# The RWKV scan of one core: the second way's tiles on the other head's partitions, its products on the off-diagonal corners of TensorE's array

## The chip, the core and the metric

The kernel runs on one core of a Trainium2 chip. The metric is the device time of one execution in microseconds (us), lower is better. The core has five engines that run on their own and wait for each other by semaphores: TensorE (PE; PEld is its weight load) multiplies, VectorE (DVE), ScalarE (ACT) and GpSimd (POOL) compute elementwise, and SyncE (SP) here only issues DMA transfers, in the order of its program.

## The reference, cut to what matters

The reference is a chain of five blocks over 512 latent and 256 context tokens of width 1024. The second layer of the last four is an RWKV layer, and the change touches its scan alone. For each of 16 heads of width 64 and each of two ways (forward and backward in time) it computes, token by token:

```
def step(S, inp):
    w_t, k_t, v_t, kk_t, a_t = inp[:5]
    s_kk = einsum('nbhvk,nbhk->nbhv', S, kk_t)
    S = S * w_t[..., None, :] - s_kk[..., :, None] * (kk_t * a_t)[..., None, :] + v_t[..., :, None] * k_t[..., None, :]
    y_t = einsum('nbhvk,nbhk->nbhv', S, inp[5])
    return S, y_t
...
y = ys[0] + flip(ys[1], axis=1)
```

## The kernel before

The scan is done in chunks of 64 tokens (CH), 12 chunks (NC) for the 768 tokens. Two heads stand together as a head pair `m` (8 pairs): head 0 on partitions 0 to 63, head 1 on 64 to 127 (`HEAD`). A pass `n` handles 4 chunks (BATCH) of one pair for both ways `d`; `pos` 0, 1, 2 is its place in the pair, and n = 3m + pos runs from 0 to 23. The second way goes through the chunks backwards (`CHUNK`).

All products of the scan are of 64x64 corners of the 128x128 array. The helper `heads` issues two of them, one for each head, with rows and output columns of the same half: the two corners on the diagonal.

In a pass, `make` on TensorE issues first the two products that VectorE masks (`sums`), then the 128-wide product of term 2 and those that turn terms by an identity, then the token products (term 2 and term 3 by the identity), then the 32x32 products of lines 3470 (`z_sums`) and 3482 (`tt_sums`), which build the inverse of a chunk's triangular matrix from two blocks, then W (`w_sums`) and the corrections (`corrected`). Between these stand the four steps (`step`) of the pass before: `new`, the state after a chunk, which VectorE scales by the chunk's decay (line 3649) and hands to the next step, and `y_sum`, the output, which VectorE adds to `y` after the fourth step (line 3658). ScalarE copies products from PSUM (line 3544). In a pair's second and third pass the layer norm of the pair before is mixed in: mean and variance (line 3506), centre (3666), squares and roots on ScalarE, reciprocals (3671) and scale (3676, 3678) on VectorE.

SP loads what a pass needs, in one queue, in this order for a pair: the blocks from which GpSimd will compute the next inverse, the terms of the first pass, the inverse (two stores to DRAM, a wait until they have landed, twelve loads), the terms of the second and the third pass. The terms of a pass are five parts, and each is issued when the one before has landed:

```
for part in range(PARTS):
    w = slice(part * LOAD, part * LOAD + LOAD)
    sp.dma_start(self.terms[b][:, w], src[:, w]).then_inc(self.landed, 16)
    sp.wait_ge(self.landed, (48 * m + 16 * b - 16) * PARTS + 16 * part + 16)
sp.sem_inc(self.ready, 1)
```

Before the first part SP waits on `taken`, by which VectorE says that the pass that used the buffer is over; three buffers are in turn. A pass on TensorE begins with a wait on `ready` (SP's line 3328). GpSimd computes the inverse of the next pair (lines 2816 to 2819, 3404) and, after `scaled`, the layer's output for a pair three back (3389, 3391).

Of the kernel before, what the change touches and what calls it, by code (L numbers as in the profile page):

```python
# [21 lines left out]
D = 1024  # L22
KD = D // P
# [24 lines left out]
CH = 64  # L48
# [3136 lines left out]
class RwkvScan(Stage):  # L3185
# [5 lines left out]
    def __init__(self, chip, before):  # L3191
# [16 lines left out]
        self.state = [chip.view(at + 2 * d * CH, 2, CH) for d in range(2)]  # L3208
        at += 4 * CH
# [9 lines left out]
        assert at <= self.masks_at, at  # L3219
        assert D + 2 * BLK * BLK <= WSLOT  # L3220
# [16 lines left out]
                "state_ready state_sums y_sums y_added made").split())  # L3237

# [64 lines left out]
    def y_sum(self, s, d):  # L3303

        return self.chip.bank(6, CH, BATCH * CH * d + CH * self.step(s, d))

    def new(self, s, d):

        return self.chip.bank(7, CH, CH * d)
# [6 lines left out]
    def sync(self, sp):  # L3316
        d, b4 = self.chip.dram, self.before
        sp.wait_ge(self.chip.stage_done, 4 * self.index)

        def terms(m, b):  # L3320
# [7 lines left out]
            sp.sem_inc(self.ready, 1)  # L3328

        def inverse(m):  # L3330
# [12 lines left out]
            for way in range(2):  # L3343
                chunks = slice(NC * way, NC * way + NC)
                for q in range(4):
                    to = slice(BLK * q, BLK * q + BLK)
# [7 lines left out]

        inverse(0)
        for u in range(2):
            sp.wait_ge(b4.bonus_stored[u], 16 * (KD // 2))
# [53 lines left out]
    def tensor(self, pe):  # L3411
# [14 lines left out]

        flat = lambda x: lambda s: x[:, s].rearrange("p n e -> p (n e)")
        at = lambda x: lambda s: x[:, s]
        id64 = lambda s: ident

        def make(n, m, pos, past):
            if n == 0:
                wait(self.before.first_terms, 16)
            else:
                wait(self.ready, n)
            for d in range(2):
                x = self.source(pos, d)
                term = lambda i: lambda s: x[:, s, i]
                if past:
                    wait(self.w_out[d], n)  # L3440
                each(at(self.half(d, 1, 0)), term(0), term(3))
                each(at(self.half(d, 1, 1)), term(3), term(1)).then_inc(self.sums[d], 1)
            for d in range(2):
                x = self.source(pos, d)
                pq = lambda s: x[:, s, 0:2].rearrange("p n e -> p (n e)")
                term = lambda i: lambda s: x[:, s, i]
                wait(self.made[d], n + 1)
                each(flat(self.slots(d, 0, 2)), term(2), pq).then_inc(self.sums[d], 1)
                each(at(self.half(d, 2, 0)), term(0), id64)
# [327 lines left out]
```

## Time and profile before

| what | value |
|---|---|
| median of 3 runs | 5429.38 us (5427.31 to 5431.54) |
| the profiled execution's span | 5432.6 us |
| share of PE busy | 88% |
| share of DVE busy | 49% |
| the scan's 64-wide products (line 3419) | 10752 records, first at 3388.7 us, last at 3905.2 us |

The profile is of one execution, whose span of 5432.6 us is its own time, 3 us above the median. All times in it count from the start of the span. PEclk is the granted share of TensorE's full clock. A product of fp32 operands leaves two matmul records and two weight loads.

### The profile page before, as it was taken

The page shows a single profiled execution, that of the slowest core. Times are in us where ns is not written, and L with a number is a line of the kernel's source. Part 1 is how long each engine was busy: PE and PEld are TensorE (multiplying, and loading weights), DVE is VectorE, ACT ScalarE, POOL GpSimd, SP SyncE. Part 2 cuts the span into 40 slices and gives each one's busy share as a digit, 9 for nine tenths or more (in the row PEclk, how much of TensorE's full clock was granted, in tenths as well). Part 3 has the DMA queues.
Part 4 walks back from the last instruction along what each step waited for, and adds up shares of the span by engine and source line. Part 5 has one row for each costly group of instructions (what it writes and reads, how often), then busy time and mean ns, then how long its engine had stood idle before and what let it go on. Part 6 is the DMA issues. An engine that isn't in the chain of part 4 may idle for free.

```text
span 5432.6 us, 72151 instructions
## 1 busy us (share of the span) xinstructions
PE 4768.6 (88%) x28910; PEld 2998.1 (55%) x28910; DVE 2667.7 (49%) x4575; ACT 1230.6 (23%) x2249; POOL 761.8 (14%) x942
## 2 busy tenths in 40 slices
PE   6987888889989989999879943899888999999998
PEld 3555734444478634555445522789744445456687
DVE  2447853441278411477565487345533444423465
ACT  2112412340011010111010164222212343301230
POOL 0004410000000000111000056656100000000000
PEclk9989998889999999999989966999998999999999
DMA  3312141012122211344103255344211100022122
GB/s 142 102 55 101 40 162 54 31 39 93 62 70 86 79 69 39 109 154 162 59 33 104 87 190 209 98 108 109 78 47 43 35 35 31 13 85 78 69 83 78
DMA packets 152502, 451.24 MB, mean 83 GB/s; under 512 B 73200, under 2 KB 73456, under 8 KB 130800
## 3 DMA queue, kind: packets, MB, share of 16 engines
q1 hardware_dynamic: 128464, 350.91, 19.1%
q0 software_dynamic: 22848, 92.29, 5.0%
q8 instruction: 231, 3.78, 0.3%
q10 hardware_dynamic: 864, 3.47, 0.2%
q14 instruction: 95, 0.78, 0.1%
HBM read 377.42 MB, written 69.21 MB: 82 GB/s over the span
## 4 chain that ended last, share of the span: by engine, by line
PE 61%; issue 9%; DVE 8%; POOLq 7%; PEld 7%; DMA 3%; ACT 2%; POOL 2%; DVEq 1%; PEldq 0%; SPq 0%; ACTq 0%
PE psum L386 50%; PEld psum L386 6%; POOLq L2819 3%; POOLq L2817 2%; PE psum L2380 2%; PE psum L2379 2%; PE psum L648 1%; PE psum L2350 1%; DVE sbuf L1091 1%; PE psum L1275 1%; DVE sbuf L663 1%; PE psum L1029 1%; PE psum L1246 1%; DVE sbuf L666 1%; DVE sbuf L1394 1%
## 5 line engine op out<-in xcount | busy, mean ns | idle before, releaser
L386 PE MATMUL psum<-sbuf 128*128 128x512 f32 (+3 forms) x10256 | 3313.4, 483 | 204.0 <-DVE sbuf L1584 52.0
L386 PEld LDWEIGHTS psum<-sbuf 128*128 128x128 f32 (+1 forms) x10256 | 1937.8, 191 | 1539.4 <-issue 1205.6
L3419 PE MATMUL psum<-sbuf 64*64 64x64 f32 (+1 forms) x10752 | 432.1, 240 | 32.2 <-SPq L3328 21.9
L3419 PEld LDWEIGHTS psum<-sbuf 64*64 64x64 f32 x10752 | 418.0, 140 | 48.9 <-SPq L3328 23.8
L598 DVE CUSTOM_DVE_ANT_0 sbuf<-sbuf 128x1024 f32<-128x1024 f32 x160 | 210.9, 1318 | 42.9 <-DMA sbuf<-w_side 27.2
L1596 DVE SCALAR_TENSOR_TENSOR sbuf<-psum,sbuf 128x256 f32<-128x256 f32 (+2 forms) x288 | 125.8, 480 | 191.1 <-PE psum L386 186.4
L3014 PE MATMUL psum<-sbuf 64*128 64x512 f32 (+2 forms) x192 | 86.5, 712 | 144.1 <-ACT sbuf L3088 66.3
L3544 ACT ACTIVATE sbuf<-psum 128x256 f32<-128x256 f32 (+3 forms) x384 | 128.4, 368 | 370.9 <-PE psum L3419 311.8
L631 ACT ACTIVATE sbuf<-sbuf 128x512 f32<-128x512 f32 (+1 forms) x114 | 52.9, 552 | 617.1 <-DVEq L3718 599.9
L588 POOL DMA_DIRECT2D sbuf<-w_side x128 | 68.4, 535 | 858.6 <-DVE sbuf L598 857.9
L2818 POOL TENSOR_TENSOR sbuf<-sbuf 96x30 f32<-96x30 f32 (+14 forms) x240 | 140.6, 586 | 50.9 <-issue 18.0
L3014 PEld LDWEIGHTS psum<-sbuf 64*128 64x128 f32 (+1 forms) x192 | 39.5, 265 | 187.0 <-POOL sbuf L2976 69.6
L1853 DVE TENSOR_TENSOR sbuf<-sbuf 128x512 f32<-128x512 f32 x40 | 27.8, 694 | 227.3 <-ACT sbuf L1843 227.3
L555 POOL DMA_DIRECT2D sbuf<-cond_rows x4 | 2.4, 603 | 940.0 <-DVEq L3718 856.8
L2816 POOL TENSOR_TENSOR sbuf<-sbuf 96x30 f32<-96x30 f32 (+14 forms) x240 | 125.9, 524 | 33.7 <-issue 1.7
L1459 DVE TENSOR_TENSOR sbuf<-sbuf,psum 128x512 f32<-128x512 f32 x16 | 10.3, 685 | 240.5 <-PE psum L386 240.5
L2524 DVE TENSOR_REDUCE sbuf<-psum 128x1 f32<-128x768 f32 x64 | 61.3, 958 | 135.8 <-PE psum L2380 134.2
L648 PE MATMUL psum<-sbuf 128*128 128x512 f32 (+1 forms) x228 | 93.0, 566 | 29.8 <-ACT sbuf L631 29.8
L3649 DVE TENSOR_SCALAR sbuf<-psum,sbuf 128x64 f32<-128x64 f32 x192 | 45.9, 280 | 147.4 <-PE psum L3419 145.8
L2477 POOL TENSOR_TENSOR sbuf<-sbuf 64x512 f32<-64x512 f32 x16 | 20.3, 1267 | 689.1 <-ACT sbuf L2412 446.1
L2380 PE MATMUL psum<-sbuf 64*128 64x512 f32 (+1 forms) x256 | 116.4, 534 | 0.0
L1584 DVE TENSOR_TENSOR sbuf<-sbuf 128x1024 f32<-128x1024 f32 (+1 forms) x100 | 100.1, 1005 | 29.0 <-DMA sbuf<-w_sgu_out 10.8
(309 smaller groups left out, 5174.2 us busy)
## 6 DMA issues: line engine op xcount, KB each, us to landing
sbuf<-w_side POOLq DMA_DIRECT2D x128, 512.0 KB, 3.9
sbuf<-w_sgu_uz SPq DMA_DIRECT2D x32, 1088.0 KB, 5.1
sbuf<-terms SPq DMA_DIRECT2D x115, 256.0 KB, 2.9
sbuf<-w_up SPq DMA_DIRECT2D x22, 1024.0 KB, 4.9
sbuf<-w_merge SPq DMA_DIRECT2D x8, 2560.0 KB, 8.9
sbuf<-w_mla_head SPq DMA_DIRECT2D x16, 1152.0 KB, 5.1
sbuf<-w_sgu_v SPq DMA_DIRECT2D x8, 2048.0 KB, 7.7
sbuf<-w_sgu_out SPq DMA_DIRECT2D x8, 2048.0 KB, 8.6
```

What stands on the lines that cost most here:

```text
L386: last = nc.tensor.matmul(out, w, x, start=(n == 0), stop=(n == len(pairs) - 1))
L598: last = v.tensor_tensor_reduce(junk, self.slot[b], self.rows[:, c], 1.0, 0.0, ALU.mult, ALU.add, self.sums[:, b, n:n + 1])
L648: last = self.nc.tensor.matmul(self.chip.bank(n, t), self.chip.const("ones"), squares[:, i], start=(i == 0), stop=(i == k - 1))
L1596: last = v.scalar_tensor_tensor(x[:, m], self.chip.bank(i)[:, cols], gates[sign][:, m:m + 1], x[:, m], ALU.mult, ALU.add)
L2379: t.matmul(s[:, a:a + w], self.qn[u][:, q], self.kn[u][:, a:a + w], start=True, stop=False)
L2380: last = t.matmul(s[:, a:a + w], rot[r, q], self.kr[u][r, a:a + w], start=False, stop=True)
L2816: engine.tensor_tensor(product, left, right, ALU.mult)
L2818: engine.tensor_tensor(x[:, j + 1:BLK, 0:j], x[:, j + 1:BLK, 0:j], product, ALU.add)
L2819: eng.drain()
L3014: last = t.matmul(out[:, at:at + width], w, x[:, at:at + width], start=True, stop=True)
L3419: last = t.matmul(out[hs], lhs[hs], rhs[hs], start=start, stop=stop)
L3544: copy = lambda to, of: a.activation(to, of, ACT.Copy)
```

## The change

The second way's (d = 1) results stand on the partitions of the other head. `heads` takes `turned`: with 1, head h is read on its own rows and written to the other half, an off-diagonal corner. The new helper `corners` issues, for each chunk, the first way's two products on the diagonal and then the second way's two off it. All products that read the terms go through it; those on already turned tiles (W, the corrections, `new`) stay on the diagonal, and the y products turn the second way back. The y products leave `step` for `outputs`, one block between W and the corrections of the next pass, and the add to `y` moves behind that pass's corrections. The states of all four steps get buffers of their own, y and state sums other places in banks 6 and 7. Since the queries and decays of the second way are read by VectorE on the partitions of the other head, SP loads them once more, crossed: `turned` behind each pass's terms, and two loads of decays at the stage's start. The inverse's loads for the second way go to swapped partitions; their number stays.

```diff
+        def turned(m, b):
+            sp.wait_ge(self.turned_in, 32 * (3 * m + b) + 32)
+            q = d["terms"][3 * m + b, :, 1].rearrange("p (c n e) -> p c n e", n=TERMS, e=CH)[:, :, 1]
+            for h in range(2):
+                sp.dma_start(self.queries[b][HEAD[h]], q[HEAD[1 - h]]).then_inc(self.turned_in, 16)
...
             sp.sem_inc(self.ready, 1)
+            turned(m, b)
...
+        for h in range(2):
+            sp.dma_start(self.decays_turned[HEAD[h]], b4.decays[HEAD[1 - h], :, 1]).then_inc(self.turned_in, 16)
         inverse(0)
+        turned(0, 0)
...
-        def heads(out, lhs, rhs, start=True, stop=True):
-            for hs in HEAD:
-                last = t.matmul(out[hs], lhs[hs], rhs[hs], start=start, stop=stop)
+        def heads(out, lhs, rhs, turned=0, start=True, stop=True):
+            for h in range(2):
+                rows = HEAD[h]
+                last = t.matmul(out[HEAD[h ^ turned]], lhs[rows], rhs[rows], start=start, stop=stop)
             return last
...
+        def corners(out, lhs, rhs, done=None):
+
+            for s in range(BATCH):
+                last = [heads(out(d)(s), lhs(d)(s), rhs(d)(s), turned=d) for d in range(2)]
+            if done is not None:
+                for d in range(2):
+                    last[d].then_inc(done[d], 1)
...
-                each(at(self.half(d, 1, 0)), term(0), term(3))
-                each(at(self.half(d, 1, 1)), term(3), term(1)).then_inc(self.sums[d], 1)
+            corners(half(1, 0), term(0), term(3))
+            corners(half(1, 1), term(3), term(1), self.sums)
...
+            corners(lambda d: flat(self.slots(d, 0, 2)), term(2), pq, self.sums)
+            corners(half(2, 0), term(0), id64)
+            corners(half(2, 1), term(4), id64, self.sums)
...
+            corners(half(0, 0), term(2), id64)
+            corners(half(0, 1), term(3), id64, self.token_sums)
...
+            if past:
+                outputs(*past)
             for d in range(2):
                 wait(self.tokens_out[d], n + 1)
                 wait(self.w_out[d], n + 1)
...
+        def outputs(n, m, pos):
+            v = self.v[pos]
             for d in range(2):
-                c = self.step(s, d)
-                heads(self.y_sum(s, d), v[d][:, c], self.nh_h[d][:, c, 0], stop=False)
-                heads(self.y_sum(s, d), self.state[d][:, s % 2], self.qa[d][:, c], start=False).then_inc(self.y_sums[d], 1)
+                wait(self.state_ready[d], 13 * m + 4 * pos + BATCH + 1)
+            for s in range(BATCH):
+                for d in range(2):
+                    c = self.step(s, d)
+                    heads(self.y_sum(s, d), v[d][:, c], self.nh_h[d][:, c, 0], turned=d, stop=False)
+                for d in range(2):
+                    c = self.step(s, d)
+                    last = heads(self.y_sum(s, d), self.state_at(n, s, d), self.qa[d][:, c], turned=d, start=False)
+                    if s + 1 == BATCH:
+                        last.then_inc(self.y_sums[d], 1)
...
-                v.tensor_tensor(self.qa[d], x[:, :, 1], c1[:, :, 0], sub)
+                if d == 1:
+                    dve.wait_ge(self.turned_in, 32 * n + 64)
+                v.tensor_tensor(self.qa[d], x[:, :, 1] if d == 0 else self.queries[pos], c1[:, :, 0], sub)
...
             dve.sem_inc(self.taken, 1)
+            if past:
+                add_outputs(*past)
```

SP's queue of DMA transfers at the start of the scan, before (line 3326 loads a part of terms, 3348 and 3349 the inverse, 3353 the blocks):

```order
L3349 DMA sbuf<-inverse 32x12x32
L3326 DMA sbuf<-terms 128x512 x5
L2953 DMA blocks<-sbuf 32x24x32 x4
L3353 DMA sbuf<-blocks 96x1024
L3326 DMA sbuf<-terms 128x512 x5
L3353 DMA sbuf<-blocks 96x1024
L3326 DMA sbuf<-terms 128x512 x5
L3339 DMA inverse<-sbuf 96x1024
L3340 DMA inverse<-sbuf 96x1024
```

and the same place of the changed kernel, where these lines are 3343 (terms), 3368 (inverse), 3372 (blocks) and 3357, 3358 (stores), and 3335 is the new load of queries:

```order
L3368 DMA sbuf<-inverse 32x12x32
L3335 DMA sbuf<-terms 64x4x64 x2
L3343 DMA sbuf<-terms 128x512 x5
L3335 DMA sbuf<-terms 64x4x64 x2
L2953 DMA blocks<-sbuf 32x24x32 x4
L3372 DMA sbuf<-blocks 96x1024
L3343 DMA sbuf<-terms 128x512 x5
L3335 DMA sbuf<-terms 64x4x64 x2
L3372 DMA sbuf<-blocks 96x1024
L3343 DMA sbuf<-terms 128x512 x5
L3335 DMA sbuf<-terms 64x4x64 x2
L3357 DMA inverse<-sbuf 96x1024
```

Two loads more stand behind each pass's terms and ahead of the next transfer: two pairs of them are ahead of the first load of blocks from which GpSimd works.

VectorE's operations from the last steps of a third pass on, before (3649 scales the states, 3658 adds to y, 3671 is a reciprocal, 3629 to 3632 take in the corrections):

```order
L3649 TENSOR_SCALAR sbuf<-psum,sbuf 128x64 x8
L3658 TENSOR_TENSOR sbuf<-sbuf,psum 128x256 x2
L3671 RECIPROCAL sbuf<-sbuf 128x384
L3629 TENSOR_TENSOR sbuf<-sbuf,psum 128x512
L3631 TENSOR_TENSOR sbuf<-sbuf,psum 128x256
L3632 TENSOR_TENSOR sbuf<-sbuf,psum 128x256
```

and of the changed kernel, where the same lines are 3695, 3705, 3718, 3670, 3674 and 3675:

```order
L3695 TENSOR_SCALAR sbuf<-psum,sbuf 128x64 x8
L3718 RECIPROCAL sbuf<-sbuf 128x384
L3670 TENSOR_TENSOR sbuf<-sbuf,psum 128x512
L3674 TENSOR_TENSOR sbuf<-sbuf,psum 128x256
L3675 TENSOR_TENSOR sbuf<-sbuf,psum 128x256
```

The add to y no longer stands between the states and the corrections; it comes after the corrections of both ways, ahead of the next pass's masks.

## Rows read from the trace of the kernel before

**Rows 1.** The page: span, TensorE, and the scan's products.
```profile
span 5432.6 us, 72151 instructions
PE 4768.6 (88%) x28910; PEld 2998.1 (55%) x28910; DVE 2667.7 (49%) x4575; ACT 1230.6 (23%) x2249; POOL 761.8 (14%) x942
L3419 PE MATMUL psum<-sbuf 64*64 64x64 f32 (+1 forms) x10752 | 432.1, 240 | 32.2 <-SPq L3328 21.9
```

**Rows 2.** Stretches: start and end, length, busy us of engines, clock, DMA.
```profile
3704.00:3764.00 60.00, 59.22 (x1619) 55.34 (x1615) 32.90 (x83) 19.60 (x57) 39.35 (x72) 1.00 0.42 112
...
3868.00:3925.00 57.00, 36.49 (x782) 32.12 (x780) 32.43 (x59) 10.25 (x25) 13.06 (x10) 0.86 0.19 67
```

**Rows 3.** Waits of 3524 to 3868 us: total, times, longest.
```profile
PE psum L3419 <- SPq L3328: 14.3, 5, 4.2
```

**Rows 4.** All waits of SP over the scan, 3388 to 3910 us.
```profile
SPq L3326 <- DMA sbuf<-terms: 257.4, 92, 4.1
SPq L3328 <- DMA sbuf<-terms: 60.9, 23, 4.0
SPq L3348 <- DMA inverse<-sbuf: 26.7, 7, 4.6
SPq L3338 <- POOLq L3405: 11.4, 1, 11.4
SPq L3334 <- DVEq L3592: 4.9, 1, 4.9
```

**Rows 5.** SP in order of time: start, us, transfers, over two head pairs.
```profile
3630.46 0.33 SPq L3353 DMA_DIRECT2D sbuf<-blocks  x1
...
3659.74 25.39 SPq L3326 DMA_DIRECT2D sbuf<-terms  x10
3688.31 0.33 SPq L3353 DMA_DIRECT2D sbuf<-blocks  x1
...
3747.77 0.33 SPq L3353 DMA_DIRECT2D sbuf<-blocks  x1
```

**Rows 6.** In order of time, TensorE and (L3605) VectorE: second passes of two pairs.
```profile
3673.80 9.43 PE L3419 MATMUL psum<-sbuf 64*64 64x64 f32 x288 [0.83 <-SPq L3328]
3683.16 0.45 PE L3470 MATMUL psum<-sbuf 32*32 32x32 f32 x32
...
3675.00 0.43 DVE L3605 TENSOR_TENSOR sbuf<-psum,sbuf 128x256 f32<-128x256 f32 x1 [0.16 <-PE psum L3419]
...
3853.51 11.01 PE L3419 MATMUL psum<-sbuf 64*64 64x64 f32 x288 [2.68 <-SPq L3328]
```

**Rows 7.** Line 3419 alone: 64-wide products only, then 128-wide ones only.
```profile
3679.00:3682.00 3.00, 3.00 (x110) 3.00 (x107) 1.00 0.34 93
3669.50:3672.50 3.00, 3.00 (x60) 3.00 (x58) 1.00 0.39 126
```

**Rows 8.** Line 3055 alone (tiles of 64 rows, 32 columns), one stretch.
```profile
3366.00:3367.00 1.00, 1.00 (x136) 1.00 (x131) 1.00 0.00 0
```

**Rows 9.** SP's issues by line: issue ns min/median/max; the parts' landing.
```profile
L3349 SPq DMA_DIRECT2D sbuf<-inverse x64: 469/471/1429, 3391.2 to 3838.9; - x64
L3326 SPq DMA_DIRECT2D sbuf<-terms x115: 319/320/1920, 3398.8 to 3865.1; - x115
DMA to landing us min/median/max: 2.5/2.9/4.5
```

**Rows 10.** The end of the scan in order of time and one group by line.
```profile
3868.19 1.43 SPq L363 DMA_DIRECT2D sbuf<-w_rwkv_out  x2
...
3876.45 0.43 DVE L3605 TENSOR_TENSOR sbuf<-psum,sbuf 128x256 f32<-128x256 f32 x1 [0.30 <-PE psum L3419]
3896.55 2.55 DVE L3671 RECIPROCAL sbuf<-sbuf 128x384 f32<-128x384 f32 x1 [0.30 <-issue]
...
3905.58 0.94 DVE L3658 TENSOR_TENSOR sbuf<-sbuf,psum 128x256 f32<-128x256 f32 x2 [0.28 <-PE psum L3419]
...
L3544 ACT ACTIVATE sbuf<-psum 128x256 f32<-128x256 f32 (+3 forms) x384 | 128.4, 368 | 370.9 <-PE psum L3419 311.8 <-PE psum L3470 30.1 <-PE psum L3482 27.9
```

More of the change, by code:

```diff
@@ L3219, in __init__ @@
         assert at <= self.masks_at, at
+        at = A_W + WSLOT + D + 2 * BLK * BLK
+        self.queries = [chip.view(at + b * BATCH * CH, BATCH, CH) for b in range(BATCHES)]
+        at += BATCHES * BATCH * CH
+        self.decays_turned, at = chip.view(at, KD, NC), at + KD * NC
+        self.state = [chip.view(at + d * 2 * BATCH * CH, 2 * BATCH, CH) for d in range(2)]
+        at += 4 * BATCH * CH
+        assert at <= A_W + 2 * WSLOT, at
         assert D + 2 * BLK * BLK <= WSLOT
@@ L3303, in y_sum, with state_at @@
     def y_sum(self, s, d):
-        return self.chip.bank(6, CH, BATCH * CH * d + CH * self.step(s, d))
+        return self.chip.bank(6 + d, CH, CH * self.step(s, d))
     def new(self, s, d):
-        return self.chip.bank(7, CH, CH * d)
+        return self.chip.bank(6, CH, BATCH * CH + CH * d)
+    def state_at(self, n, s, d):
+        i = BATCH * n + s
+        return self.state[d][:, i % (2 * BATCH)]
     def step(self, s, d):
@@ L3453, in make @@
             for d in range(2):
-                x = self.source(pos, d)
-                term = lambda i: lambda s: x[:, s, i]
                 wait(self.evacuated[d], 2 * n + 2)
-                each(at(self.half(d, 0, 0)), term(2), id64)
-                each(at(self.half(d, 0, 1)), term(3), id64).then_inc(self.token_sums[d], 1)
+            corners(half(0, 0), term(2), id64)
+            corners(half(0, 1), term(3), id64, self.token_sums)
             if past:
@@ L3537, in alone @@
                 step(*past, s)
+            outputs(*past)
             mean(KD - 1)
@@ L3639, in begin @@
                 for d in range(2):
-                    v.memset(self.state[d][:, 0], 0.0)
+                    v.memset(self.state_at(n, 0, d), 0.0)
                     dve.drain().then_inc(self.state_ready[d], 1)
@@ L3647, in step, with add_outputs @@
             for d in range(2):
-                at = m * (2 * NC) + NC * d + self.step(s, d) + self.CHUNK[pos][d]
-                v.tensor_scalar(self.state[d][:, 1 - s % 2], self.new(s, d), self.decays[:, at:at + 1], None, mult
+                at = self.step(s, d) + self.CHUNK[pos][d]
+                decay = (self.before.decays[:, m, 0] if d == 0 else self.decays_turned[:, m])[:, at:at + 1]
+                v.tensor_scalar(self.state_at(n, s + 1, d), self.new(s, d), decay, None, mult
                                 ).then_inc(self.state_ready[d], 1)
-            if s + 1 == BATCH:
-                if n == 0:
-                    dve.wait_ge(self.zeroed, 1)
-                for d in range(2):
-                    dve.wait_ge(self.y_sums[d], 4 * n + 4)
-                for d in range(2):
-                    y = self.y[:, m * NC + self.CHUNK[pos][d]:m * NC + self.CHUNK[pos][d] + BATCH]
-                    v.tensor_tensor(y, y, self.chip.bank(6, BATCH * CH, BATCH * CH * d).rearrange("p (c e) -> p c e", e=CH), add).then_inc(self.y_added[d], 1)
-                    dve.drain()
+        def add_outputs(n, m, pos):
+            if n == 0:
+                dve.wait_ge(self.zeroed, 1)
+            for d in range(2):
+                dve.wait_ge(self.y_sums[d], n + 1)
+            for d in range(2):
+                y = self.y[:, m * NC + self.CHUNK[pos][d]:m * NC + self.CHUNK[pos][d] + BATCH]
+                v.tensor_tensor(y, y, self.chip.bank(6 + d, BATCH * CH).rearrange("p (c e) -> p c e", e=CH), add).then_inc(self.y_added[d], 1)
+                dve.drain()
         def centre(m):
@@ L3684, in alone @@
                 step(n, m, pos, s)
+            add_outputs(n, m, pos)
             centre(m)
```

28 lines of the change are left out of this document (12 added, 16 removed).

## The prediction, made blind

> **What bounds the kernel now.** I read the page first, for how much of the span the scan's products are. Line 3419 holds all 64-wide products of the scan, 10752 matmul records busy 432 us, first at 3388.7 us and the last at 3905 us [rows 1]. Everything the change touches lies in this stage of some 537 us, a tenth of the span. A product of fp32 operands leaves two records, so these are 5376 products over 24 passes.
>
> Then the stretches. TensorE is busy 59.22 of 60.00 us between 3704 and 3764, at the full clock [rows 2]. That invites the reading that the products set the pace. The list of waits warns against it: between 3524 and 3868 TensorE's longest waits end at SP's line 3328, 14.3 us in 5 times [rows 3]. Line 3328 is where SP says that a pass's terms have landed.
>
> So I read SP's own waits, and this is what decides [rows 4]. Over the scan SP waits 257.4 + 60.9 us for its own loads of terms and 26.7 us for its own stores of the inverse. It waits only once each for another engine: 11.4 us for GpSimd's first inverse and 4.9 us for VectorE's memset. It never waits for `taken`, the semaphore by which the passes would hold it back. In order of time the same shows [rows 5]: a head pair is a load of blocks, five parts of terms one after the other, two stores and twelve loads of the inverse, then ten parts. The next load of blocks comes 57.9 us later (3630.46 to 3688.31) and the one after that 59.5 us later. Nothing in between is idle but landing time. SP runs free at some 58 to 60 us a head pair, and TensorE needs a little less: its three passes fit, with 0.83 us of waiting at 3673.80 and 2.68 us at 3853.51, each at a pair's second pass, the one behind the loads of the inverse [rows 6]. Two chains stand almost level, and SP's is the slower one.
>
> **The change, part by part.**
>
> *Products on all four corners.* A 64-wide product on the diagonal costs 3.22 us / 110 = 29.3 ns a record (a 3 us stretch that holds 110, the last one running 0.22 us over), a 128-wide one 3.27/60 = 54.5 ns [rows 7]. Two corners take turns. The trace has no four corners of 64x64. The nearest row is line 3055: tiles of 64 rows and 32 columns, of which two share each half of the rows, in the same order of halves as the new code. At full clock 136 records overlap 1.00 us, 1.19/136 = 8.8 ns each [rows 8]. Line 3470, with four 32x32 tiles that share no rows, takes (0.45-0.19)/31 = 8.4 ns [rows 6]. So sharing rows costs nothing there. I take half of today's spacing for corners: 14.7 and 27.3 ns. Per pass 192 records of 64 columns, 32 of 128 and the 64 records of y move to corners: 2.8 + 0.9 + 0.9 = 4.6 us less TensorE work in a pass. The bounds are 0 (no overlap) and 5.9 us (spacing down to line 3055's).
>
> The Trainium skill speaks against this ("TensorE: Matmul & The Clock Gate", Part 3): a weight load overlaps products in flight only where its row group differs, and an off-diagonal corner shares its rows with a diagonal one. By that rule the corners would gain nothing; line 3055's spacing here disagrees, for 32 columns. It is a rival below.
>
> *SP gets two more loads in each pass.* `turned` stands behind each pass's terms and ahead of all that SP does next: 64 partitions x 4 runs of 256 bytes, 256 runs, twice. SP's issue of a part of terms (128 runs) takes 0.32 us, of an inverse load (384 runs) 0.47 us, both with outliers to 1.9 us [rows 9]. I take 0.42 us with its gap, so 0.84 for two, 0.1 for the semaphore steps (`turned` waits for the pair before it, landed long ago), and 0.3 because the next part queues behind 512 small runs (parts land in 2.5 to 4.5 us, 2.9 in the median, so a little more traffic is felt). That is 1.25 us a pass. Bounds: 0.75 (twice 0.32 and the steps) and 1.9.
>
> Which of them count? Those of passes 4 to 22 stand after SP's one wait for GpSimd and ahead of the last pass's terms: 19 x 1.25 = 23.8 us. Those of passes 0 and 1 stand ahead of the load of blocks from which GpSimd makes the first inverse, on which SP waits 11.4 us, so they pass through: 2.4 us. Those of passes 2 and 3 vanish in that wait. The two loads of decays lie in the 4.9 us that SP waits for the memset. The last pass's terms land 26.2 us later (bounds 15.8 and 40).
>
> *y products in one block, late; add to y after the corrections.* They leave the four steps of state and stand between W and the corrections. Cover: SP's 15.6 us or more between passes. In the last pass and the steps after it they are bare.
>
> *What is given back at the end.* Today SP's last terms are in at 3868.2 (its next load goes out then), while VectorE's first mask of the last pass is at 3876.45, and it follows the start of the pass by 1.2 us as at 3673.80 to 3675.00 [rows 6, 10]. The pass starts at 3875.2, 7.0 us late, because TensorE lags. Shorter passes take this lag away where they fit between SP's arrivals: the second pass of a pair gets 15.6 us (14.3 + 1.25). I lay a pass out by durations of today [rows 10]. After 1 us of first products, eight masks and evacuations of up to 0.43 us on VectorE hold the token products back to 3.7 us, ScalarE's copies of 0.37 us hold z to 6 us, the small products with their copies, variance and roots end at 10.3, W 1.75, y 0.9, corrections 3.45: 16.4 us. I leave 1.5 us of lag. VectorE then needs 1.2 + 0.94 (the moved add) + 2.55 (reciprocal): 21.1 us, where it is 23.9 today (3875.2 to 3899.1, where today's reciprocal ends). So 2.8 us less. The y products of the last batch cost 1.8 us more behind the last state: 64 records at twice 14.7 ns, since TensorE idles between these steps and the granted clock of this stretch averages 0.86, part of it at the lower of the two levels, 1.2 GHz in place of 2.4 [rows 2]. Given back: 7.0 - 1.5 + 2.8 - 1.8 = 6.5 us (bounds 3 and 10).
>
> **The sum.** 26.2 - 6.5 = 19.7 us more. The profiled execution has a span of 5432.6 us, 3 us above the median of 5429.4, and the difference carries over: 5449 us. The middle of the scan gains nothing: where a pass takes 16 us in place of 19, TensorE waits longer at SP's line.
>
> **The rivals.**
>
> *Corners that don't overlap*: the second product on a half of the rows waits for the first, passes stay at 19 us, TensorE keeps its lag, SP's 18 x 1.25 + 2.4 = 24.9 us reach the 22nd pass, which today already waits for its terms (2.68 us), and all behind it shifts alike, with 1.8 us of y on top: +26.7, 5456 us. Against it: line 3055. For it: nothing in this trace has 64-column weights on shared rows at this pace. Chance 0.10. The rule of the Trainium skill quoted above would have it so.
>
> *The loads are cheap*: 0.8 us a pass and 9 us given back, 16.8 - 9 = +8 us, 5437 us, within what can be told. For it: the 0.32 us issues. This and smaller mixtures: 0.27.
>
> *The products set the pace after all*, the other side: were SP not the slower chain, each pass would lose some 3.5 us, 24 x 3.5 = 84 us, 5345 us. For it speak the 59.22 of 60.00 busy us. The point from which it decides: SP's three sets of terms, inverse and extra loads would have to take under the 47 us of three shortened passes, and they take 58 and more. For a gain that can be measured at all, `turned` would have to cost under 0 us beside the lag, or the parts land 0.3 us sooner each. Chance 0.07, and 0.02 for small gains.
>
> *Cold TensorE*: gaps at each first pass grow to some 10 us (z waits for the inverse, about 16 us behind the terms), and after idle stretches like that of 3868 to 3925 the granted clock averages 0.86 [rows 2]. A cold last pass would take back up to 6 us. This lies inside my forecast's range.
>
> **How the numbers follow.** My forecast, SP's chain longer and part of it given back, has 0.54 and by itself 5440 to 5462. What a measurement of this kernel tells from no change is about 0.2%, 11 us. Slower by over that: 0.54 + 0.10, less 0.02 for its edge, 0.62. Within: 0.29. Faster: 0.09. The range 5431 to 5466 leaves out the fast case, the dearest loads (40 - 3 = +37) and little else.
>
> **What would show it.** SP's loads of blocks 61 to 64 us apart, in place of 58 to 60, and still no wait for `taken`. TensorE's busy time in the scan down by some 100 us, its waits that end at SP's ready line between the second inverse and the last terms up from 14.3 us to over 60. Records of corner products half as far apart. Passes in step with SP: the last one starting within 2 us of the last terms. It would be wrong if SP waited for passes, if the query loads' issue took under 0.3 us each, or if part loads went faster with TensorE idle.

## The result, and the profile after

The changed kernel takes 5465.9 us (median; runs of 5460.0 to 5467.9 us) against 5428.4 us for the kernel before in the same job. The ratio is 1.0067, with a 95% interval of 1.0054 to 1.0081: slower by some 36 us (the two medians are 37.5 us apart). One more execution of it, and one of e2 below, ran at a granted clock under 0.7 (8757 and 6946 us) and are left out. The forecast was 5449 us and the range 5431 to 5466: the time lies inside by 0.1 us, and the loss is nearly twice the 19.7 us that were forecast.

The page of the kernel after answers to [rows 1]. SP's waits and TensorE's waits over the scan answer to [rows 4] and [rows 3]. The lines are renumbered: 3343 is the wait for a part of terms (3326 before), 3345 that for the last part (3328), 3335 the new query loads, 3356 the wait for GpSimd, 3372 the load of blocks (3353), 3442 the 64-wide products (3419), 3498 the product z with the inverse (3470), 3536 the sums of mean and variance (3506).

```profile
span 5466.1 us, 72297 instructions
L3442 PE MATMUL psum<-sbuf 64*64 64x64 f32 (+1 forms) x10752 | 348.1, 248 | 77.6 <-SPq L3345 21.6
```

SP's own waits, 3380 to 3960 us: engine and line, what it waited for, us in total, times, longest.

```profile
SPq L3343 <- DMA sbuf<-terms: 259.1, 92, 6.0
SPq L3345 <- DMA sbuf<-terms: 59.5, 23, 4.0
SPq L3367 <- DMA inverse<-sbuf: 24.4, 7, 3.9
SPq L3356 <- POOLq L3427: 7.7, 1, 7.7
```

TensorE's waits in the same stretch:

```profile
PE psum L3498 <- DMA sbuf<-inverse: 56.0, 8, 14.7
PE psum L3442 <- SPq L3345: 21.6, 10, 5.6
PE psum L3442 <- issue: 19.0, 17, 3.0
PE psum L3442 <- DVE sbuf L3652: 15.8, 17, 1.7
```

Read together: SP waits for the same things for the same time as before and never for `taken`, so it still runs free. The products are 84 us less busy (348.1 for 432.1), and TensorE stands still for all of it and for the 31 us by which the stage is longer. SP in order of time shows what is new in its round:

```profile
3581.62 0.60 SPq L3372 DMA_DIRECT2D sbuf<-blocks  x1
...
3648.01 0.62 SPq L3335 DMA_DIRECT2D sbuf<-terms  x1
3648.67 0.60 SPq L3372 DMA_DIRECT2D sbuf<-blocks  x1
...
3666.11 1.25 SPq L3335 DMA_DIRECT2D sbuf<-terms  x2
3667.41 0.61 SPq L3357 DMA_DIRECT2D inverse<-sbuf  x1
...
3709.80 0.60 SPq L3372 DMA_DIRECT2D sbuf<-blocks  x1
```

A query load takes 0.6 us to issue, two of them hold the queue for 1.30 us (3666.11 to 3667.41), and the load of blocks that follows takes 0.60 us where it took 0.33 [rows 5]. The blocks are 67.1 and 61.1 us apart.

The stage's end, TensorE in order of time (start, us, records, in brackets the idle time ahead and what ended it):

```profile
3909.46 0.69 PE L3442 MATMUL psum<-sbuf 64*64 64x64 f32 x32 [0.76 <-DVE sbuf L3652]
3913.13 1.97 PE L3442 MATMUL psum<-sbuf 64*64 64x64 f32 x48 [2.97 <-issue]
3915.03 0.65 PE L3498 MATMUL psum<-sbuf 32*32 32x32 f32 x32
...
3917.46 2.42 PE L3536 MATMUL psum<-sbuf 128*128 128x384 f32 x4
...
3936.52 1.12 PE L3442 MATMUL psum<-sbuf 64*64 64x64 f32 x16 [0.73 <-DVE sbuf L3695]
3938.37 1.99 PE L3442 MATMUL psum<-sbuf 64*64 64x64 f32 x64 [0.73 <-DVE sbuf L3695]
```

And as stretches (length, then busy us of TensorE, its weight loads, VectorE, ScalarE, GpSimd; granted clock; DMA). Before, the last pass from its first record to VectorE's last subtraction, then from there to the stage's end (the first addition of line 1584):

```profile
3875.16:3896.24 21.08, 19.54 (x520) 18.01 (x516) 11.55 (x28) 6.22 (x18) 2.93 (x3) 1.00 0.13 44
3896.24:3924.42 28.18, 9.83 (x136) 7.79 (x136) 14.57 (x21) 1.72 (x3) 8.32 (x6) 0.72 0.08 28
```

After:

```profile
3904.63:3928.07 23.44, 18.38 (x516) 15.93 (x516) 11.32 (x28) 6.02 (x18) 1.21 (x3) 0.85 0.36 131
3928.07:3961.34 33.27, 12.29 (x136) 8.02 (x136) 15.41 (x22) 1.72 (x3) 8.32 (x6) 0.57 0.07 24
```

The last pass is 2.4 us longer and what follows it 5.1 us longer, each at a lower clock than before.

**The account.** SP has the last pass's terms in at 3904.5 us, 36.8 us later than before. 5.4 us of that lie ahead of the scan, in code that the change leaves alone (the scan began at 3394.1 in place of 3388.7 in these two executions), so SP's chain is 31.4 us longer. TensorE's lag at the last pass is gone (it starts 0.1 us behind its terms, 7.4 before): -7.3. Last pass +2.4, tail +5.1. Sum +31.6, and the stage ends 31.5 us later against its start. The rest of the 36 us is of the size by which the code ahead varies between executions.

### The profile page after: what moved, and what is told of

Its sections match the earlier page's. It is cut to its first block, busy times and chain, and to the rows that moved or that the text cites. A ratio compares the mean times of both kernels' runs of the same rounds, so it can differ in the third digit from the quotient of the medians.

```text
span 5466.1 us, 72297 instructions
## 1 busy us (share of the span) xinstructions
PE 4703.1 (86%) x28910; PEld 2920.8 (53%) x28910; DVE 2665.7 (49%) x4575; ACT 1226.1 (22%) x2249; POOL 764.1 (14%) x942
## 4 chain that ended last, share of the span: by engine, by line
PE 60%; issue 10%; DVE 8%; POOLq 7%; PEld 7%; DMA 3%; ACT 2%; DVEq 1%; POOL 1%; PEldq 1%; SPq 0%; ACTq 0%
PE psum L386 48%; PEld psum L386 6%; POOLq L2819 3%; POOLq L2817 2%; PE psum L2380 2%; PE psum L2379 2%; PE psum L648 1%; PE psum L2350 1%; DVE sbuf L1091 1%; PE psum L1275 1%; DMA sbuf<-w_side 1%; DVE sbuf L663 1%; PE psum L1029 1%; PE psum L1246 1%; DVE sbuf L666 1%
## 5 line engine op out<-in xcount | busy, mean ns | idle before, releaser
L3442 PE MATMUL psum<-sbuf 64*64 64x64 f32 (+1 forms) x10752 | 348.1, 248 | 77.6 <-SPq L3345 21.6
L3442 PEld LDWEIGHTS psum<-sbuf 64*64 64x64 f32 x10752 | 329.0, 145 | 102.3 <-issue 37.5
```

The costliest lines, as they stand in the source:

```text
L3442: last = t.matmul(out[HEAD[h ^ turned]], lhs[rows], rhs[rows], start=start, stop=stop)
```

## The experiments

The theory: SP's serial queue sets the pace, the query loads lengthen it, and all that the corners save turns into waiting. The rival: the off-diagonal corners, the order of the products or the late y products are what costs. In the table, *pass* is the mean distance of VectorE's first masks from pass 5 to pass 23, *tail* the time from the end of VectorE's last subtraction to the stage's end, both from the profiled execution.

| kernel | median us | ratio to before, 95% | pass us | tail us |
|---|---|---|---|---|
| before | 5428 to 5433 | | 20.36 | 28.2 |
| after | 5465.9 | 1.0067 (1.0054 to 1.0081) | 21.31 | 33.3 |
| e1 after, no query loads | 5435.1 | 1.0006 (0.9997 to 1.0015) | 19.75 | 32.7 |
| e2 before, with the loads | 5468.1 | 1.0066 (1.0053 to 1.0079) | 22.08 | 27.3 |
| e3 after, parts in flight | 5421.9 | 0.9979 (0.9970 to 0.9989) | 19.57 | 33.3 |
| e4 before, parts in flight | 5413.2 | 0.9967 (0.9954 to 0.9980) | 20.04 | 28.3 |
| e5 after, loads on ScalarE | 5432.7 | 1.0004 (0.9995 to 1.0013) | 20.37 | 32.9 |
| e6 = e3 and e5 | 5419.7 | 0.9983 (0.9974 to 0.9992) | 19.92 | 32.6 |
| e7 = e6 on the diagonal | 5434.3 | 1.0009 (0.9999 to 1.0019) | 20.19 | 34.4 |
| e8 = e6, way by way | 5416.2 | 0.9972 (0.9961 to 0.9982) | 19.41 | 32.9 |
| e9 after, filled tail | 5461.3 | 1.0050 (1.0034 to 1.0065) | 21.48 | 29.0 |
| e10 after, y in its steps | 5456.0 | 1.0039 (1.0024 to 1.0055) | 21.85 | 31.0 |
| e11 = e8, e9 and e10 | 5410.0 | 0.9959 (0.9946 to 0.9973) | 19.28 | 28.4 |
| e12 = e4 and filled tail | 5412.8 | 0.9961 (0.9948 to 0.9975) | 20.11 | 26.7 |

**e1: the loads taken out of the change.**

```diff
             sp.sem_inc(self.ready, 1)
-            turned(m, b)
...
         inverse(0)
-        turned(0, 0)
...
```

> The changed kernel without the two query loads that SP issues in each pass; VectorE takes the queries from the other half of the partitions, so the second way's output is of the wrong queries, and the work on every engine stays the same. The loads of the turned decays stay. Theory (SP's serial queue sets the pace, and each pass's two query loads lengthen it by 1.3 us): the last pass's terms are in 24 to 28 us earlier than in the changed kernel (3904.49 us there), the loads of blocks are again 57 to 60 us apart, and the time falls to 5438 to 5442 us. Rival 1 (off-diagonal corners, the interleaving or the later y products cost the time): the loads of blocks come as now, or the passes hold SP, and the time stays above 5460 us. Rival 2 (all is the loads, and the end gives back the 6.5 us of the prediction once SP is free): 5430 us or less.

Measured: 5435.1 us, the time of the kernel before within what can be told, and 2.9 us below my 5438 to 5442. SP's loads of blocks, in order of time, are 60.1 and 59.5 us apart and take 0.33 us again:

```profile
3568.54 0.33 SPq L3371 DMA_DIRECT2D sbuf<-blocks  x1
...
3628.60 0.33 SPq L3371 DMA_DIRECT2D sbuf<-blocks  x1
...
3688.05 0.33 SPq L3371 DMA_DIRECT2D sbuf<-blocks  x1
```

Rival 1 falls: with corners, order and late y products in place and the query loads gone, the loss is gone. The last terms come 36.7 us sooner (3867.8), more than the 24 to 28 I gave it; 2.6 us of that lie ahead of the scan, so SP's chain is 34.1 us shorter. Rival 2 falls too: with SP free there is no gain either. The end takes it: from the last pass's first mask to the stage's end it takes 54.2 us, as after the change (54.5), where the kernel before takes 48.0.

**e2: the loads alone, on the kernel before.**

```diff
...
             sp.sem_inc(self.ready, 1)
+            turned(m, b)
...
+        for h in range(2):
+            sp.dma_start(self.decays_turned[HEAD[h]], b4.decays[HEAD[1 - h], :, 1]).then_inc(self.turned_in, 16)
         inverse(0)
+        turned(0, 0)
...
+                dve.wait_ge(self.turned_in, 32 * n + 64)
```

> The kernel before with nothing added but the new loads: two of decays ahead of the scan, two of queries behind each pass's terms, from the same place in SP's program into tiles that nothing reads; VectorE waits for them as in the changed kernel. Theory: SP's chain to the last terms grows by the 31 us of the changed kernel. TensorE's lag of 7 us at the last pass is used up, since its passes of 19 us fit between arrivals that are 20 us apart or more, but the end keeps its old length: 24 to 31 us more, 5452 to 5459 us. Rival 1 (the corners or their order are what costs): within 8 us of the kernel before, under 5437 us. Rival 2 (the shorter passes do give time back in the changed kernel, by 6.5 us or more): above 5470 us.

Measured: 5468.1 us, the whole loss of the change, with nothing of it but its loads. It is above my 5452 to 5459. In this execution SP's blocks were 68.4 and 63.3 us apart:

```profile
3574.52 0.60 SPq L3366 DMA_DIRECT2D sbuf<-blocks  x1
...
3642.91 0.60 SPq L3366 DMA_DIRECT2D sbuf<-blocks  x1
...
3706.19 0.60 SPq L3366 DMA_DIRECT2D sbuf<-blocks  x1
```

From the third load of blocks on, where the queue runs free, a pair takes 65.2 us on average, against 60.1 in the kernel before and in e1, 63.9 after the change, and 65.6 and 65.9 in e9 and e10, which leave SP's program alone. Measured from the scan's start to the last terms, SP's chain is 31.4 us longer than before after the change, 31.8 and 38.4 us in e9 and e10, and 41.2 us in e2. The loads' price differs from execution to execution. With e1 the sign is settled from both sides: the loads cost the 0.7%, the rest of the change costs or gives nothing that can be told.

**e3 and e4: SP's chain of landings cut short, on either kernel.** The five parts of a pass's terms are issued one behind the other.

```diff
             for part in range(PARTS):
                 w = slice(part * LOAD, part * LOAD + LOAD)
                 sp.dma_start(self.terms[b][:, w], src[:, w]).then_inc(self.landed, 16)
-                sp.wait_ge(self.landed, (48 * m + 16 * b - 16) * PARTS + 16 * part + 16)
+            sp.wait_ge(self.landed, (48 * m + 16 * b) * PARTS)
```

> The changed kernel with the five parts of a pass's terms issued one behind the other and one wait for all, in place of a wait behind each. Theory (SP's chain of landings sets the pace and hides what the corners give): SP needs some 6.5 us for a pass's terms in place of 14, its three sets with the inverse and the query loads take 40 us, TensorE's passes of 16 us become the pace (48 us a pair), and the time falls by 60 to 90 us, to 5375 to 5405 us. Rival (the transfers themselves are the limit, and parts in flight together land later by as much): within 15 us of the changed kernel, 5450 us or more.

> The kernel before with the same edit: five parts of terms in flight, one wait. It says what a pass takes when SP is not the bound, on the diagonal. Theory (two chains nearly level, TensorE's passes at 19 us, 57 us a pair against SP's 58 to 60): 8 to 20 us faster than before, 5408 to 5421 us, with SP now waiting for `taken`; the gap to the changed kernel with the same edit is what the corners give, 20 to 45 us. Rival (the corners do not overlap, or their order costs): the changed kernel with this edit is no faster than this one.

Measured: 5421.9 and 5413.2 us. SP now waits for the passes in both. In e3:

```profile
SPq L3345 <- DMA sbuf<-terms: 108.4, 23, 6.5
SPq L363 <- PEq L1576: 100.4, 1, 100.4
SPq L3343 <- DVEq L3678: 96.5, 11, 11.8
```

The wait for VectorE's `taken` (line 3678) is there, 11 times, and SP reaches the next stage's loads so early that it waits 100 us there. For e4 the time is as the theory said (5408 to 5421), but not what was to follow from it: the changed kernel was to be 20 to 45 us faster than e4, and it is 8.7 us slower. That is the outcome which the rival named, though not for its reason: the corners do overlap. For e3 the theory fails, and with it a step of my thinking: with SP out of the way the shorter passes were to set a pace of 16 us, 5375 to 5405 us. They came 19.6 us apart, against 20.0 on the diagonal. The corners gave 0.5 us a pass, 8.5 us from pass 5 to pass 23. e4 is still the faster kernel: it reaches pass 5 in 112.3 us from the scan's start, e3 in 122.2, and its last pass and tail are 2.9 us shorter. The rival I named (transfers as the limit) is not it either, since SP waits for the passes.

**e5 and e6: the query loads on ScalarE's queue.** e5 on the changed kernel, e6 with the parts in flight as well.

```diff
-            turned(m, b)
...
                 copy(self.mg_g[d][:, :, 1], self.half(d, 0, 1)).then_inc(self.tokens_out[d], 1)
+            turned(n, pos)
             for d in range(2):
                 act.wait_ge(self.z_sums[d], n + 1)
```

> The changed kernel with its two query loads of a pass issued from ScalarE's queue, behind the token copies, in place of SP's; the loads of the turned decays stay on SP. Theory (only what SP's queue issues counts): the loads of blocks are 57 to 60 us apart again and the time is that of the kernel without the query loads, 5433 to 5441 us; ScalarE's 1.2 us of issue a pass stands ahead of its copy of z and is hidden by the wait for SP. Rival 1 (the transfers themselves cost, whoever issues them): the parts of terms land later, and the time stays above 5455 us. Rival 2 (ScalarE's issue lies on the passes' own chain): 5445 us or more with SP's loads of blocks as in the kernel before.

> The changed kernel with both edits: the parts of terms in flight together, and the query loads on ScalarE's queue. The passes set the pace here. In the changed kernel with the parts in flight alone they came 19.6 us apart, with TensorE 80% busy. Theory (a pass is a chain over TensorE, VectorE and ScalarE, and the corners shorten only TensorE's share): SP's start is some 6 us earlier without the query loads ahead of the first load of blocks, the passes stay at 19.5 to 20 us, 5408 to 5420 us. Rival 1 (SP's issues still hold the passes there): passes 17 us apart or less, under 5395 us. Rival 2 (ScalarE's 1.2 us of issue is on the passes' chain): passes 20.5 us or more, above 5430 us.

Measured: e5 5432.7 us, 0.3 us below its 5433 to 5441. The same bytes move, and against the kernel before nothing is lost that can be told: it is the place in SP's queue that costs nearly all, and hardly the transfer. Not quite nothing: from the third load of blocks on a pair takes 61.1 us on average (60.2 to 62.5, where I had put 57 to 60), 1.0 us more than in e1, which has no such loads. e6 5419.7 us, passes 19.9 us apart: as the theory said, and within what can be told of e3.

**e7 and e8: what the corners are worth where SP does not hold the passes.** e7 is e6 with the second way on the diagonal; e8 keeps the corners of e6 and runs the ways one after the other.

```diff
...
-                last = t.matmul(out[HEAD[h ^ turned]], lhs[rows], rhs[rows], start=start, stop=stop)
+                last = t.matmul(out[rows], lhs[rows], rhs[rows], start=start, stop=stop)
...
```

```diff
-            for s in range(BATCH):
-                last = [heads(out(d)(s), lhs(d)(s), rhs(d)(s), turned=d) for d in range(2)]
+            last = [None, None]
+            for d in range(2):
+                for s in range(BATCH):
+                    last[d] = heads(out(d)(s), lhs(d)(s), rhs(d)(s), turned=d)
```

> The same kernel as the one with both edits, but the second way stays on its own head's partitions and on the diagonal corners: the order of the products, the loads (now of the same partitions) and the waits are those of the changed kernel. Its difference to that kernel is what the off-diagonal corners give when SP does not hold the passes. Theory (corners take 3.5 us of TensorE's time out of a pass, and the waits for VectorE and ScalarE put in some 3): passes 1 to 3 us further apart than with corners, 5435 to 5480 us. Rival (the longer products cover the masks and copies, as in the kernel before): passes within 0.5 us of those with corners, within 12 us of its time.

> The kernel with both edits and the second way on the off-diagonal corners, but each group of products runs all of the first way and then all of the second, in place of step by step in turn. It says whether it is the taking of turns that lets the corners overlap. Theory (two corners at a time take turns as on the diagonal): corner records 29 ns apart as in the kernel before, TensorE's busy time back to some 420 us, and a time within 8 us of the kernel on the diagonal with the same edits. Rival (off-diagonal corners are themselves faster or slower): records under 20 ns, or over 32 ns, apart.

Measured: e7 5434.3 us, between theory and rival: 14.6 us behind e6, where the rival allowed 12 and the theory began at 5435 us, but with passes of 20.2 for 19.9 us, the rival's. The products by line, 3380 to 3925 us (busy us, mean ns, then idle time ahead of them and its main releasers), e6 first and e7 below:

```profile
L3434 PE MATMUL psum<-sbuf 64*64 64x64 f32 (+1 forms) x10752 | 336.9, 243 | 71.2 <-DVE sbuf L3651 24.2 <-issue 23.8 <-DVE sbuf L3694 10.8
```

```profile
L3434 PE MATMUL psum<-sbuf 64*64 64x64 f32 (+1 forms) x10752 | 422.4, 237 | 28.7 <-DVE sbuf L3694 11.3 <-issue 5.9 <-DVE sbuf L3712 3.5
```

On the corners the line is 85.5 us less busy and 42.5 us more idle. TensorE also waits 17.6 us more at z (36.0 for 18.4) and is 9.5 us more busy in the sums at line 3528 (36.8 for 27.3), which the lower clock slows. These three make 70 us. From its first product to its end the stage takes 528.1 us in e6 and 536.2 us in e7, 8.1 us in all, so some 77 of the 85 us are given back inside it. The rest of the difference between these two executions, 4.7 us, lies ahead of the scan, in code that is the same. By what ended TensorE's idle time in the stage, two causes are the largest: stalls of issue (39.7 us over all lines, 10.4 in e7) and waits for VectorE's masks (24.2 us at line 3651), which the second way's longer products had covered.

e8 is my clear miss: 5416.2 us, no slower than e6, and 18 us from e7; the products' line is busy 353.9 us, where I had put 420. In it 80 records of 64 columns take 1.86 us, 20.8 ns from one start to the next, where I expected 29 and the rival under 20 or over 32:

```profile
3681.85 1.86 PE L3434 MATMUL psum<-sbuf 64*64 64x64 f32 x80 [1.45 <-DVE sbuf L3653]
```

The single starts of the records say more than their mean. In the kernel before they come in twos: two starts 7 ns apart, the next two 58.4 ns behind (from 3679 us on: 37, 44, 95, 102, 154, 160 ns). The two diagonal corners don't take turns, as the prediction and e8's expectation had it; they start together. After the change they come in fours at the same distance (from 3904.63 us on: 169, 174, 180, 187, then 227, 232, 239, 245 ns). In e8 both twos and fours stand in the same row. So the second way's records can start while the first way's are still in work, over more than the record next in line; the rows don't say which way a record belongs to. Taking turns step by step is not needed.

**e9 and e10: the tail.** e9 fills TensorE's waits behind the last pass with products that nothing reads; e10 puts the last batch's y products back behind its steps, in banks that are free by then.

```diff
+        def fill(k, bank=1):
+            for i in range(k):
+                heads(self.chip.bank(bank, CH), ident, ident)
+
         def alone(*past):
+            fill(16)
             for s in range(BATCH):
                 step(*past, s)
+                fill(4)
             outputs(*past)
+            fill(6)
             mean(KD - 1)
+            fill(12, 0)
             variance(KD - 1)
```

```diff
             for s in range(BATCH):
                 step(*past, s)
-            outputs(*past)
+                for d in range(2):
+                    c = self.step(s, d)
+                    heads(self.last_sum(s, d), v[d][:, c], self.nh_h[d][:, c, 0], turned=d, stop=False)
+                for d in range(2):
+                    c = self.step(s, d)
+                    last = heads(self.last_sum(s, d), self.state_at(n, s, d), self.qa[d][:, c], turned=d, start=False)
+                    if s + 1 == BATCH:
+                        last.then_inc(self.y_sums[d], 1)
...
```

> The changed kernel with filler products on TensorE in the waits after the last pass only: 16 pairs ahead of the first of the four steps, 4 behind each step, 6 behind the y products, 12 behind the mean, into PSUM that nothing reads. In the changed kernel steps 1 to 3 of the tail run 54 ns a record, the y products 26.6 ns, the mean's products 0.64 us apart, all at the lower clock. Theory (the lower clock comes from TensorE's idle time and costs some 4 us there): the granted clock between the last corrections and the stage's end rises from 0.61 to over 0.9, the y products run at 14.6 ns and the mean's at 0.32 us, the time from the end of the last corrections to the stage's end (34.1 us now, from 3927.19 to 3961.26) falls by 3 to 5 us. Rival (the clock is set by something else, or the tail hangs on VectorE alone): clock and length as they are, within 1 us.

> The changed kernel with the y products of the last batch back behind each of its four steps, into two PSUM banks that are free by then; everything else as changed. Theory (in the tail the moved y products are bare: 16 records behind each step are covered by VectorE's turn, in one block they cost 1.7 us at the lower clock and a hand-over): last corrections to the stage's end 1.5 to 2.5 us shorter than in the changed kernel (34.1 us), steps still 1.85 us apart, the time itself within what can be told of the changed kernel. Rival (the block costs nothing): within 0.5 us of 34.1 us.

Measured from the end of VectorE's last subtraction to the stage's end, e9:

```profile
3927.71:3956.71 29.00, 12.09 (x308) 9.61 (x303) 15.45 (x22) 1.72 (x3) 8.32 (x6) 0.86 0.08 29
```

e10:

```profile
3929.00:3960.00 31.00, 11.38 (x136) 7.32 (x136) 15.58 (x22) 1.72 (x3) 8.32 (x6) 0.54 0.08 26
```

Both lengths are as the theory said. Filled, the tail is 4.3 us shorter and the clock 0.86 for 0.57 (I had put it over 0.9); its steps lie 1.42 us apart in place of 1.85, the sums 0.32 us apart in place of 0.64. With y in the steps it is 2.3 us shorter at an unchanged low clock. The whole times, 5461.3 and 5456.0 us, are lower than after's by 4.6 and 9.9 us; for e10 that is more than its tail explains, while its profiled scan was longer, and the intervals of its ratio and of after's touch. What lies between is not settled.

**e11 and e12: the best of both kinds.**

> All that helped, on the off-diagonal corners: parts of terms in flight together, query loads on ScalarE's queue, the ways one after the other within a group, the last batch's y products in its steps, filler products in the tail. Against the same kernel without the last two (5416 us) the tail is 3 to 6 us shorter: 5409 to 5415 us. Rival (the fillers delay the steps): 5416 us or more.

> The kernel before, on the diagonal, with the parts of terms in flight together and filler products in the tail (16 pairs ahead of the steps, 6 behind them, 12 behind the mean). Against the same kernel without fillers (5413 us, last mask to stage's end 48.2 us) steps 1 to 3 at full clock end nothing sooner where VectorE's turn covers them, so 0 to 4 us less: 5409 to 5413 us. If the corners are worth their price with everything else mended, the kernel on the corners with the same edits beats this one; by the runs so far they are level.

Measured: 5410.0 and 5412.8 us, both as expected, 0.41% and 0.39% faster than before, and level with one another. The corners and their extra loads are worth nothing that can be told even with everything else mended; one line, the parts of terms in flight, gives nearly all of the gain to the kernel before.

e12's tail serves as a measure for e9's. With fillers the old order of work takes

```profile
3887.94:3914.65 26.71, 10.56 (x237) 8.29 (x232) 14.56 (x20) 1.72 (x3) 8.32 (x6) 0.82 0.09 31
```

against 28.3 us without them (e4, granted clock 0.73). So fillers give the old order 1.6 us and the changed one 4.3 us, and with fillers in both the changed tail is still 2.3 us longer (29.0 for 26.7).

## Why the prediction was right, and where it was off

- **The range held by luck.** The two halves of the sum were 26.2 us of longer loads and 6.5 us given back; measured from the scan's start in the profiled execution they are 31.4 us and nothing (-0.2 us); the first lies inside its bounds of 15.8 and 40, the second outside its bounds of 3 and 10. The range was wide enough for both by 0.1 us.
- **The bound** was right: SP runs free, with no wait for `taken`; e1 and e2 show it from both sides. My "58 to 60 us" a pair left out a pair of 63.1 us (3567.39 to 3630.46 in the kernel before). From the third load of blocks on, the pairs went from 60.1, 63.1, 57.9 and 59.5 us to 62.9, 67.0, 61.1 and 64.7: 3.8 us more a pair on average, three times 1.27.
- **The loads' price in the steady state** was right for this execution: 24.5 us from the second inverse load to the last terms, 23.8 foretold (19 x 1.25). An issue took 0.61 us where I took 0.42, and what stands behind it less than I gave it. In other executions of the same SP program it was higher, up to 5.8 us a pair (e10). So the rival of cheap loads, 0.8 us a pass, fell.
- **The loads' price at the start** was mis-sized. I had 2.4 us for passes 0 and 1 and nothing for passes 2 and 3 and the decays; it was 7.0. The wait for GpSimd that was to swallow it fell from 11.4 to 7.7 us, but the load that GpSimd waits for is itself behind them.
- **"Given back: 6.5 us"** is the term that failed: the lag was given back (7.3 us, where I had asked for 5.5), and then lost. From its first record to the end of its reciprocal the last pass was to take 21.1 us in place of 23.9 and took 27.4: 3.5 us longer, with one stall of issue of 2.97 us and with z, W and the sums at the lower clock. From there to the stage's end it was to be 1.8 us longer and was 4.0. Cut at the last subtraction instead, the tail is 5.1 us longer. With fillers in both orders (not placed quite alike: e9 has some between the steps too) 2.3 us of that are left, which is also what e10 finds for y's place; the other 2.8 us go with the lower clock.
- **The stall in the last pass came back.** All five profiled executions on the corners with the parts chained (after, e1, e5, e9, e10) have stalls of issue of 2.3 to 3.6 us in their last pass, which takes 20.2 to 22.5 us from first mask to last subtraction, against 19.8 before. e3, e6, e8 and e11, with the parts in flight, have 0.8 us or less of it there and take 17.7 to 19.0 us. So the pass does get 1 to 2 us shorter where the stall is absent. In the five, SP's 2 MB of weights for the next stage move during the last pass, in the four they moved before it; whether that brings the stall is not shown. My rival "cold TensorE" held the clock, priced at up to 6 us and put inside the range; it should have been in the forecast, for the gaps that it needs were in the forecast.
- **Corners overlap**: right in the number, half of today's spacing. 64 records of corner products lie within 1.00 us (below), where 64 at 29.3 ns took 1.9 us [rows 7]. The picture behind it, that two corners take turns, was wrong: two start together, and now four. TensorE's busy time at the line fell by 84 us where I had put some 100, part of it because more of the stage ran at the lower clock (0.87 for 0.95 granted from 3395 to 3905 us).
- The rule of the Trainium skill that I set against it ("TensorE: Matmul & The Clock Gate", Part 3: a weight load overlaps products in flight only where the row group differs) did not hold for corners that share their rows.
- **"The products set the pace"** (5345 us) fell twice: SP was the bound, and e3 shows that with SP out of the way passes do not shrink to 16 us either. My own "passes fit in 16.4 us" was the same error in the forecast. I added up busy times and single durations and left out that shorter products uncover VectorE's and ScalarE's part of the same pass, and that stalls of issue grow (31.8 us in the changed kernel's stage, 4.9 before).
- **TensorE's waits at SP's ready line over 60 us**: wrong in its place. Between the second inverse and the last terms they fell from 14.3 to 8.6 us (over the whole scan 21.9 before, 21.6 after). The new idle time stands at z, for the inverse (56.0 us in 8 waits, 13.5 before), at the masks and at issue.

## What to carry to other kernels

Before an engine's work is made cheaper, look at which queue of transfers runs free beside it. Here two loads added to a serial queue that waits for each landing cost some 36 us in all, and the same loads on a queue with slack (ScalarE's) cost nothing that could be told. Don't count on a pass over three engines to shrink by what one of them saves: here 85 us less of products made the stage 8 us shorter, for two streams of work cover each other's latencies. Measure it with the outer bound removed first. And look at work that is moved to the end of a stage: here the y products stood bare there, behind idle time and at the lower clock, and cost 2.3 us.

## What the runs showed of the hardware

- Products on four 64x64 corners of the array start together, also in pairs on the same rows: four records within 18 ns every 58.4 ns, where the diagonal alone had two. That is 14.6 ns a record in place of 29.3 [rows 7]; here 64 within one us:

```profile
3904.63:3905.63 1.00, 1.00 (x64) 1.00 (x64) 1.00 0.00 0
```

- The number of runs alone doesn't set how long a DMA's issue holds its queue: 0.32 us for 128 runs on 128 partitions and 0.47 us for 384 on 32 [rows 9], but 0.61 us for a query load of 256 on 64. The forecast's 0.42 us lay between the first two. The next issue behind a query load is slower too (0.60 for 0.33 us).
- TensorE stands still for 2 to 3 us now and then with nothing that it waits for ("issue"); shorter products have more of it (23.8 us in e6, 5.9 in e7, at the line of the products). In e6 one stands ahead of the record at 3689.47. Of q8, a DMA queue that the profile calls "instruction", the 5 us before it hold no packet, and the 2.6 us around the stall hold one:

```profile
3689.47 0.27 PE L3434 MATMUL psum<-sbuf 64*64 64x64 f32 x1 [2.29 <-issue]
```

```profile
q8 instruction: 1, 0.02, 2.6%
```

  The same holds for every such stall over 1.2 us in the scan: in all 11 after the change and all 15 in e6, a packet of q8 starts 2.2 to 3.0 us ahead of the stall's end, though these packets come only every 5 us or so. The DMA engines can be full (the stall of 2.97 us in the last pass) or nearly idle meanwhile (5% at 3846). That TensorE runs out of instructions there fits all of this, but no run took it apart.
- Filler products raised the granted clock of the changed tail from 0.57 to 0.86 and made it 4.3 us shorter; in the old order they raised it from 0.73 to 0.82 and gave 1.6 us.
